# A third modulation and K moved among the steps of a gated recurrence, on one Trainium2 core

## The reference, cut to what matters

```python
h = rms_norm(x, gain) * (1 + scale_m) + shift_m            # the modulation: silu(c) @ w_ada + b_ada
hq, hf, hi, hg, fq, fk, fv, ff = split(h @ w_in)           # 7 x 512 columns, and 8 columns of logits (ff)
logf, k = gates(hf); b = cumsum(logf)                      # per head and channel
for each block of rows:                                    # the recurrence, 4 heads of 128
    o = (q*exp(b)) @ S + causal(q, k, exp(b_t - b_s)) @ v
    S = exp(b_last) * S + (k*exp(b_last - b)).T @ v
logf_fox = log_sigmoid(ff + bias); c = cumsum(logf_fox)    # forgetting attention, 8 heads of 64
p = softmax(fq @ fk.T / 8 + c_q - c_k); fox = p @ fv
x = x + gate_m * (concat(norm(o)*silu(hg), norm(fox)) @ w_out)
y = rms_norm(x + gate_f * moe(rms_norm(x)...))             # 16 experts, two for each row
```

## Time and profile before

| | |
|---|---|
| median of 3 runs | 776.3 us (773.58 to 778.24) |
| the profiled execution | 772.52 us, of which the span from first to last instruction is 770.7 us |
| mean granted TensorE clock | 0.942 of full |
| busy: PE / DVE / ACT / POOL | 664.5 / 384.5 / 210.3 / 214.8 us |
| DMA | 182.95 MB, mean 237 GB/s |

### The profile page before, as it was taken

How to read it: one execution, slowest core, us unless ns; L and a number is a source line. 1 busy time by engine, 2 the same in 40 slices (tenths; PEclk the granted TensorE clock), 3 DMA queues, 4 the chain that set the end, 5 groups by cost and what they waited for, 6 DMA issues and landing times. The chain is left out here.

```text
span 770.7 us, 19144 instructions
## 1 busy us (share of the span) xinstructions
PE 664.5 (86%) x7487; PEld 439.4 (57%) x7487; DVE 384.5 (50%) x1055; ACT 210.3 (27%) x425; POOL 214.8 (28%) x336
## 2 busy tenths in 40 slices
PE   3999999999976968998899992699999999999920
PEld 1686476444442857765764552566666666676710
DVE  4200024200399787675645438455555555555556
ACT  5210137000341132266501110123232322232203
POOL 1212100100396620131100000234354444444440
PEclk9999999999989889999899996699999999999975
DMA  8963082536304110391095129699999999999724
GB/s 337 400 269 109 1 328 91 239 113 256 128 2 133 53 31 2 133 344 72 6 397 244 55 82 359 256 417 414 415 415 414 415 409 413 406 413 408 262 73 184
DMA packets 38417, 182.95 MB, mean 237 GB/s; under 512 B 5912, under 2 KB 6312, under 8 KB 22672
## 3 DMA queue, kind: packets, MB, share of 16 engines
q1 hardware_dynamic: 29968, 158.88, 52.2%
q0 software_dynamic: 8384, 23.12, 8.3%
HBM read 169.57 MB, written 15.28 MB: 240 GB/s over the span
## 5 line engine op out<-in xcount | busy, mean ns | idle before, releaser
L1758 PE MATMUL bank<-weights,x_hT 128*128 128x512 f32 x256 | 113.4, 602 | 0.0
L1742 PE MATMUL bank<-x_hT,weights 128*128 128x272 f32 x384 | 91.1, 398 | 0.0
L2047 PE MATMUL bank<-weights,R 128*32 128x256 f32 x1408 | 80.6, 379 | 4.8 <-issue 3.6
L1758 PEld LDWEIGHTS bank<-weights,x_hT 128*128 128x128 f32 x256 | 48.8, 193 | 60.4 <-issue 60.2
L1742 PEld LDWEIGHTS bank<-x_hT,weights 128*128 128x128 f32 x384 | 73.5, 193 | 16.2 <-issue 0.8
L844 POOL DMA_INDIRECT y_d<-R,x_hT x44 | 50.9, 1156 | 96.1 <-DVE R L1570 46.4
L2047 PEld LDWEIGHTS bank<-weights,R 128*32 128x32 f32 x1408 | 54.0, 110 | 28.2 <-issue 6.8
L1086 ACT ACT_TABLE_LOAD x44 | 56.5, 1283 | 21.0 <-DVEq L1189 20.3
L838 POOL DMA_INDIRECT R<-h_d,x_hT x46 | 48.0, 1044 | 45.7 <-POOL x_hT L857 26.6
L1086 ACT ACTIVATE R<-bank 128x128 f32<-128x128 f32 x44 | 12.2, 278 | 175.2 <-PE bank L2047 175.2
L1976 PE MATMUL bank<-weights,x_hT 128*128 128x512 f32 x128 | 58.3, 608 | 0.0
(11 more groups left out here) (346 smaller groups left out, 990.7 us busy)
## 6 DMA issues: line engine op xcount, KB each, us to landing
weights<-in_w_ada SPq DMA_DIRECT2D x24, 1024.0 KB, 11.0
weights<-in_w_exp_gate SPq DMA_DIRECT2D x16, 1024.0 KB, 11.1
weights<-in_w_exp_down SPq DMA_DIRECT2D x16, 1024.0 KB, 11.2
weights<-in_w_exp_up SPq DMA_DIRECT2D x16, 1024.0 KB, 11.1
R<-in_w_exp_down SPq DMA_DIRECT2D x16, 1024.0 KB, 11.0
weights<-in_w_in SPq DMA_DIRECT2D x7, 2048.0 KB, 8.9
R<-in_w_exp_up SPq DMA_DIRECT2D x8, 1024.0 KB
R<-in_w_exp_gate SPq DMA_DIRECT2D x8, 1024.0 KB, 10.9
```

What stands on the lines that cost most here:

```text
L1742: ins = T.matmul(bank[b][:, 0:HALF], w[:, k, h * P:(h + 1) * P], hT[:, k, c * HALF:(c + 1) * HALF], start=(n == 0), stop=(n == KT - 1))
L1758: ins = T.matmul(bank[b][:, :], hT[:, k, i * P:(i + 1) * P], w[:, k, :], start=(k == 0), stop=(k == KT - 1))
L2047: ins = T.matmul(bank[2][32 * j:32 * j + 32, 0:2 * P].rearrange("p (w f) -> p w f", w=2), XT[:, k, :], W2[:, :, k, j * P:(j + 1) * P], sta ...
```

## The change

1. The last third of the modulation, `ada2`, comes early: its halves stand after the second and the fourth head of hf, ahead of hi, and its bias add on DVE (and the store on POOL) ahead of the copies of hi. To make its pieces arrive, the second third `ada1` comes before and after hg.
2. K, its transposes and the logits go into `schedule`, between the steps. K is now in banks 6 and 7 and its transposes in bank 3. Step -1 (attention for tile 0) comes right after hi, and V comes after step 1.
3. On DVE the copies of hi are split, three ahead of the operands of tile 0 and two after; ACT's and DVE's work on K and the logits follows the table.
4. On SP the load of fv waits for Db0 and that of fq for Db2. On POOL the stores of K and V move between the `exponents`, and the first `exponents` no longer wait for a hi tile, since they stand behind the store of `ada2`.

Nothing is computed that was not computed before, and nothing is left out.

```diff
-        schedule = [("fv", i) for i in range(NTILE)] + [("fq", h, c) for h in range(4) for c in range(2)]
-        for step, after in reversed(list(zip(range(-1, NTILE), (1, 4, 6, 8, 10, 11)))):
-            schedule.insert(after + 1, ("hgrn", step))
-        schedule.insert(1, ("lfT",))
+        schedule = [("hgrn", -1), ("fk", 0), ("fk", 1), ("fkT", 0), ("hgrn", 0), ("fk", 2), ("fkT", 1), ("ff",), ("fk", 3), ("fkT", 2),
+                    ("fk", 4), ("lfT",), ("fkT", 3), ("fkT", 4), ("hgrn", 1), ("fv", 0), ("fv", 1), ("hgrn", 2),
+                    ("fv", 2), ("fv", 3), ("fv", 4), ("fq", 0, 0), ("hgrn", 3),
+                    ("fq", 0, 1), ("fq", 1, 0), ("fq", 1, 1), ("fq", 2, 0), ("hgrn", 4), ("fq", 2, 1), ("fq", 3, 0), ("fq", 3, 1)]
...
-        ring += [("hf", 6, 2), ("hi", 4, 2)] + [(f"ada1_{k}", k - 4, 1) for k in range(4, 8)]
-        ring += [("fk", 6, 2)] + [(f"ada2_{k}", k, 1) for k in range(4)]
-        ring += [("fv", 4, 2)] + [(f"ada2_{k}", k - 4, 1) for k in range(4, 8)]
-        ring += [("fq", 6, 2)]
+        ring += [("hf", 6, 2)] + [(f"ada1_{k}", k - 4, 1) for k in range(4, 8)]
+        ring += [("hi", 4, 2)] + [(f"ada2_{k}", k % 4, 1) for k in range(8)]
+        ring += [("fk", 6, 2), ("fv", 4, 2), ("fq", 6, 2)]
...
-        for r, first in enumerate(("hT00", "hf00", "fk0")):
+        for r, first in enumerate(("hT00", "hg0", "hf20")):
...
+                    if name == "fv":
+                        filled(sp, "Db0")
+                    if name == "fq":
+                        filled(sp, "Db2")
...
-            taken(pool, "hi0")
             exponents(0)
             exponents(1)
             pool.dma_start(S_sample, a["state_hgrn"].rearrange("l b h k v -> k (l b h) v")).then_inc(s_S0, 16)
+            filled(pool, "Db0")
+            exponents(2)
+            store_k(0)
+            store_k(1)
+            filled(pool, "Db1")
+            exponents(3)
+            store_k(2)
+            store_k(3)
+            filled(pool, "Db2")
+            exponents(4)
...
+            ada(1, 1, 0, 4)
             loaded(pe, "hg")
             for i in range(NTILE):
                 token_major("hg", i, 2 + i % 2)
-            ada(1, 1, 0, 4)
-            feature_major("hf")
             ada(1, 1, 4, KT)
+            feature_major("hf", range(2))
+            ada(2, 0, 0, 4)
+            feature_major("hf", range(2, 4))
+            ada(2, 0, 4, KT)
             loaded(pe, "hi")
```

More of the change, by code:

```diff
@@ L196, in build @@
             grp(f"hg{i}", 2 + i % 2, "act")
+        grp("ada1", 1, "dve")
         for h in range(HGH):
@@ L755, in _ @@
             both(pool, s_kout)
+            filled(pool, "fkT4")
             pool.dma_start(ckB.rearrange("p h t -> p (h t)"), bcast(ck_d.rearrange("h t -> (h t)"), P)).then_inc(s_ckr, 16)
[L757 to L764, removed]
+            for i in range(NTILE):
+                store_v(i)
             filled(pool, "fv4")
@@ L947, in _, with evict_k @@
                 A.activation(kk[:, h, :], fr, ACT.Exp).then_inc(s_kk, 1)
-            for i in range(NTILE):
+            def evict_k(i):
                 n = ROWS[i]
@@ L986, in _ @@
             for item in schedule:
+                if item[0] == "fk":
+                    evict_k(item[1])
+                if item[0] == "ff":
+                    taken(act, "ff")
+                    alink(act, A.activation(ssel[0:8, 0:TOK], cf[0:8, 0:TOK], ACT.Abs))
+                    alink(act, A.activation(ssel[0:8, 0:TOK], ssel[0:8, 0:TOK], ACT.Exp, scale=-1.0))
+                    A.activation(ssel[0:8, 0:TOK], ssel[0:8, 0:TOK], ACT.Ln, bias=1.0).then_inc(s_ln, 1)
                 if item[0] == "fq":
@@ L1267, in _ @@
             filled(dve, "hT41")
+            dve.wait_ge(s_badd, 64)
+            filled(dve, "modT")
+            filled(dve, "ada1")
+            read("dve", "ada1", V.tensor_tensor(msb, bank[1][:, :], badd, ALU.add))
             for h in range(HGH):
@@ L1282, in _, with evict_v @@
                 vlink(dve, ins)
[L1283 to L1287, removed]
+            dve.wait_ge(s_badd, 96)
+            dve.wait_ge(s_modw, 32)
+            filled(dve, "ada2")
+            read("dve", "ada2", V.tensor_tensor(msb, bank[0][:, :], badd, ALU.add))
+            def evict_v(i):
                 filled(dve, f"hi{i}")
@@ L1295, in _ @@
                     read("dve", f"hi{i}", ins)
[L1296 to L1303, removed]
             known = {"le": 0}
@@ L1329, in end_operands @@
                 V.tensor_tensor(kE[i % 2][:, :, 0:n], kE[i % 2][:, :, 0:n], kk[:, :, t0:t0 + n], ALU.mult).then_inc(s_qk, 1)
[L1332 to L1337, removed]
-            read("dve", "lpT", V.tensor_copy(lf[0:8, SEQ:SEQ + PAST], bank[2][0:8, 0:PAST]))
@@ L1348, in _ @@
+            for i in range(3):
+                evict_v(i)
             dve.wait_ge(s_qs, HGH)
@@ L1351, in _ @@
             end_operands(0)
+            for i in range(3, NTILE):
+                evict_v(i)
             for n in range(2):
@@ L1399, in _ @@
             for item in schedule:
+                if item[0] == "fkT":
+                    i = item[1]
+                    n = ROWS[i]
+                    filled(dve, f"fkT{i}")
+                    read("dve", f"fkT{i}", V.tensor_copy(fkT[:, :, i * P:i * P + n], bank[3][:, :].rearrange("p (a b) -> p a b", a=4)[:, :, 0:n]))
+                if item[0] == "ff":
+                    fox_sums()
                 if item[0] == "lfT":
@@ L1744, in feature_block, with feature_major @@
                 end(f"{name}{h}{c}", ins)
-            def feature_major(name):
+            def feature_major(name, heads=range(4)):
                 loaded(pe, name)
-                for h in range(4):
+                for h in heads:
                     for c in range(2):
```

107 lines of the change are left out of this document (56 added, 51 removed).

## The result

The changed kernel took 763.1 us (median of 4 runs, 760.1 to 763.7), the kernel before 774.9 beside it (4 runs, 771.2 to 778.2): a ratio of 0.9845, 95% interval 0.9818 to 0.9873. The forecast was 763.9.

What follows compares the result with a forecast made beforehand. Bound by the recurrence's exchange between DVE, ACT and TensorE, with too little projection work beside it. Losses of 16 us against 28.4 start the attention 12.4 earlier, at 312.6: 763.9 against the 776.3 median; forecast 759 to 768 (0.50), range 755 to 773.

Steps and rivals of the forecast that it cites:

- The sum: TensorE from hi's end (168.7) to the forgetting attention: 127.9 us of work plus 16 lost, against 28.4 lost before.
- first transpose of K: After step -1, TensorE waits for ACT's copy of the first K tile: 2.4 us lost, bounds 0.3 and 12.6.
- wait at `lfT`: After the small K tile, `lfT` waits for bank 3 until DVE copies K's third transpose behind the logits: 7.7 us.
- two transposes behind it: Two transposes following `lfT` in the same bank each wait for DVE's copy: 1.5 us.
- later steps: Steps 1 to 3, with 14 us or more of V or Q beside each on TensorE: 1 us for all.
- tile 0: Operands of tile 0 from POOL and DVE ready about when hi ends: cost 0 to 0.5, 0.4 in the sum.
- lower clock and the rest: TensorE's clock falls after the `lfT` wait, during attention for tile 2: 3 us, bounds 1 and 6.
- One of my signs: Sign that the prediction is right: the first transpose of K waits 1 to 4 us for ACT.
- `ada2`'s pieces: The last piece lands at 137.6, needed at 138.4 on TensorE: 0 us lost, bounds 0 and 3.
- Copies and products: DVE's four copies and 14 products in a full step: 9.7 us taken, bounds 7.7 and 20.
- second rival: DVE's copies take 8.4 us in both full steps, 4.4 more each; gain 3.6, time 772.7; chance 0.24.
- third rival: DVE's copies and products take 20 us in each of two steps; 36.6 lost, time 784.5; chance 0.08.

Runs made afterwards that it cites:

- e: From the changed kernel, only `lfT`, the transposes of the logits, moved behind the first V tile; 762.3 us, ratio 0.9842.
- a_logits_late: From the changed kernel, logits moved between V tiles 2 and 3, `lfT` behind the second Q block; 760.7 us (0.9826), run again 762.8 (0.9865).
- c: From the changed kernel, the second half of `ada2` and its bias add put behind hi again, K left among the steps; 781.7 us, ratio 1.0080.
- f: From the changed kernel, K and logits put back ahead of the recurrence and the loads not held, modulation still early; 764.1 us, ratio 0.9859.
- g: From a_logits_late, outputs and state put between the two halves of the next tile's pair products on TensorE; 762.3 us, ratio 0.9854.
- d: From the changed kernel, the loads of fv and fq no longer wait for Db0 and Db2; 764.7 us, ratio 0.9869.
- j: From g, K's transposes copied by ScalarE instead of VectorE, ScalarE's end factors placed between its copies of K; 756.0 us, ratio 0.9779.

## Why the prediction was right, point by point

**The sum.** TensorE's work after `hi` was put at 127.9 us and the loss at 16.0. Measured: `hi` ends at 170.39, the attention starts 144.41 later, so 16.5 are lost. That the total fits to half a microsecond is in part luck, as the terms show. The start of the attention was forecast at 312.6 and came 2.2 later: `hi` ended at 170.39 instead of 168.7. With the 1.4 us behind it the traces show 8.8 us of gain, where 12.4 were forecast. In the medians the gain is 11.8 (774.9 less 763.1): the profiled execution is the slowest of its four, and that of the kernel before lies 2.4 below its median. That the 763.9 is met within a microsecond is luck of that kind too.

| term | predicted | measured |
|---|---|---|
| first transpose of K | 2.4 | 0.43 |
| wait at `lfT` | 7.7 | 6.25 |
| two transposes behind it | 1.5 | 0.57 + 0.88 |
| later steps | 1 | 0.56 |
| tile 0 | 0.4 | 0 |
| stops amid small products | not in the sum | 1.86 + 2.22 |
| third transpose of K | not in the sum | 1.36 |
| lower clock and the rest | 3 | 2.4 (16.5 less the waits) |

**What was mis-sized.** The first two terms came out 3.4 too high, and 5.4 us of waits were left out. The two belong together: each stop holds TensorE up, so it comes later to the point where it would have waited for ACT or DVE. At the first transpose ACT's copy came 1.6 us later than forecast (190.3 for 188.7), TensorE 3.5 later (189.9 for 186.4), of which 1.7 are hi's and 1.86 the stop. The third transpose waits because VectorE copied the second by 217.1 and not by 213.2. One of my signs did not show: the first transpose was to wait 1 to 4 us and waited 0.43. Two stops with "issue" as their releaser were in the trace of before too; I had read only waits that end on an engine:

```profile
226.96 0.69 PE L1835 MATMUL bank<-weights 128*32 128x32 f32 x34 [1.65 <-issue]
...
297.57 0.22 PE L1835 MATMUL bank<-x_hT 128*32 128x32 f32 x2 [2.25 <-issue]
```

**What was right.** The place of the largest wait and its cause, the copy of K's third transpose behind the logits in VectorE's queue: shown by e (the wait moves to whatever next wants the bank) and by a (without the logits ahead of it, it shrinks). `ada2`'s pieces came in time; POOL started at 147.4 against 148.5. Copies and products took 10.2 and 10.4 against the 9.7 that I chose between 7.7 and 20. The copies at 2.1 us agree with what the Trainium skill (SBUF — State Buffer, "Who interferes with whom") would allow for four lock-outs by instructions of 0.6 us; the second rival's 8.37 appears in no row of the changed kernel. I had put that row down to POOL's start inside the copies, and the runs bear this out: where a stream of 128x256 subtractions begins inside them they take 8.37 (before) and 9.29 (c), beyond that allowance, so there the measurement decides; wherever such a stream is already running they take 1.95 to 2.1. The third rival, at 20 us for a step, didn't come either.

**What the prediction didn't separate.** It summed the change as one. The runs show that the early modulation carries it (f: 0.9859 by itself; c: 1.0080 without it), that K's new place exchanges a wait before the state for one at `lfT`, and that with the loads held the stop of step -1 is 2.6 us shorter, a gain that the times don't resolve. The forecast was right for the whole; a forecast for K's move alone from the same rows would have credited it with too much: my expectation of f gave the early modulation 3 to 6 us without it, and 9.7 came (773.8 less 764.1).

**Left open.** What TensorE waits for in the stops is not named by any row. That they are its instructions arriving is argued from three things: three of four vanish when larger matrix products stand between (g), one grows when a load fills the DMA engines (d), and two packets of the instruction queue move in that stretch of the changed kernel, 170 to 180 us (queue: packets, MB, share):

```profile
q8 instruction: 2, 0.03, 1.4%
```

Their times (near 172.8 and 176.4) don't coincide with the ends of the stop, 173.5 to 175.4, so it stays an argument. Nor does it say why the same products had no stop in step 2 of the changed kernel. Why POOL's start inside the copies holds them until its stream is all but through, and a start ahead of them does not, no row tells. Why two executions of a_logits_late differ in clock between 195 and 230 is open too.

## What to carry to other kernels

When a chain of engines starts late because something that it does not read stands ahead of it, moving that ahead can be worth more than reshuffling the filler work: here it brought 1.4 of the 1.6%. POOL's subtractions read nothing of the modulation; they stand behind its store in POOL's queue, and those of tile 0 write into the two slots of `weights` in which pieces of `ada2` had lain. Whether another order of that queue, with other slots, would do as well was not tried. When a wait ends on a copy, read what stands ahead of that copy in its engine's queue, and look for an engine that is idle there: moving the copies, with the end factors beside them, gained what moving the work between the copies could not (j against g). And read the waits that end on nothing: a stop of 2 us delays the engine to the next wait, so removing the stops alone (g) showed no gain.

## What had not been expected of the hardware

Amid the small products of a step, 208 of 32 columns and 8 of 64, TensorE stops for 1.1 to 2.5 us in many steps, though not in all; in d, under a load, for 4.46. Four copies of 32x128 on VectorE took 8.37 and 9.29 us where GpSimd's stream of 128x256 subtractions began while they ran, and 1.95 to 2.1 where it was already running. After 6.25 us of standing still TensorE's clock was at 0.50 from 225 to 236.5, though TensorE had been fully busy from 230 on; after a wait of 3.46 (a_logits_late) it stayed at 1.00, and after one of 1.95 in the second run of that kernel it was at 0.66 from 215 to 220.
